# Weights of the merge and output products split once, ahead of the last stage, and its first inputs loaded before it begins

## The chip, the cores and the metric

One core of a Trainium2 chip (five engines: PE or TensorE, DVE or VectorE, ACT or ScalarE, POOL or GpSimd, SP or SyncE, and 16 DMA engines that serve the queues of SP and ACT). The metric is the device time of one execution in microseconds; less is better.

## The reference

One layer of a decoder trunk over 2048 tokens and 1024 channels, in float32. The input is normalised and modulated, projected to 8704 columns, and these columns feed four mixers (pooling, a gated linear recurrence, a short convolution, differential attention) and their gates. What follows is the part that the last stage of the kernel computes:

```python
gates = jax.nn.sigmoid(m_g.reshape(B_, T, N_BRANCH, D))
merged = (gates[:, :, 0] * (y_pool @ w_merge_pool[l])
          + gates[:, :, 1] * (y_hgrn @ w_merge_hgrn[l])
          + gates[:, :, 2] * (y_conv @ w_merge_conv[l])
          + gates[:, :, 3] * (y_diff @ w_merge_diff[l]))
out = merged @ w_out[l]
x = x + gate[:, None] * rmsnorm(out, g_post[l])
```

The branch outputs have 256, 256, 256 and 512 channels, ten blocks of 128 together.

## The kernel before, in words

**Split products.** Every large product is made from operands that are split in two: a high part, rounded to PE's fast 32-bit format (an ACT copy), and a low part, the rest (a DVE or POOL subtraction). Three products stand for one: high by high, high by low, low by high.

**The trunk** (`trunk`, from L124) makes the input projection. Its work is cut into 476 products in slots 0 to 475, twelve matmuls of 128x512 each (L1682 to L1684), 238 for each half of the tokens. In the first half the weights of `w_in` are loaded by SP (`load_w1`, `load_w2`) into `w1` and `w2_0`, `w2_1`, split by ACT (`high`) and DVE (`low`) and stored; in the second half ACT only reloads the stored parts (L933), so `w1` and `w2` have no user there. Each engine has one program, a loop over the slots that is written out, with the mixers and the attention placed in it by slot numbers (second half: attention from slot 284 over 71 slots). A result leaves PSUM by ACT (L949) or DVE (L1250) and SP stores it, gates into the scratch tensor `gT` (L414), branch outputs into `yT`. At the end SP waits until all is stored, and a barrier of all engines parts the trunk from the last stage.

**The last stage** (`merge_and_output`, L1906) goes over four groups of 512 tokens. A group has eight merge steps `d`, one for each 128 channels of the merged result, and then four output blocks `b` of 128 tokens.

In a merge step PE makes 30 matmuls into four PSUM banks, one for each branch (L2222 to L2224): ten blocks of the branch output `y` by the weights `wm` of this `d`, three products each. DVE multiplies each bank with its gate (L2095), POOL adds the four (L2054, L2056), ACT copies the high part of the sum (L2154, `high`), DVE subtracts for the low part (L2084, `low`). DVE's order is fixed: `low(n - 1)` stands between the second and the third multiplication of step `n`. So a step's last two multiplications wait for the POOL and ACT work on the step before.

The weights of a step are loaded anew in every group, four DMAs of rows of 512 bytes, 0.66 MB together (L1977), two buffers, two steps ahead; ACT and DVE split them again each time (`split_wm`: L2130, L2075). The gates of a step are one DMA of 1.05 MB (L1985) in rows of 2 KB out of four planes of `gT` that lie 8 MB apart; four buffers, sigmoid on ACT (L2148).

In the first group `w_out` comes in besides (`load_wo`, L1997), eight blocks of 0.5 MB, split by ACT (L2166) and POOL (L2059); the first output product waits for the last of them.

An output block is 48 matmuls (L2208 to L2210) into one of two banks `pb`. ACT takes the mean square (L2183) and its root, DVE scales (L2113), POOL adds `x` (L2064), SP stores. The ten `y` blocks of the next group are loaded one after the other (L1991, two buffers), from the last merge step on, and split by ACT and DVE (L2144, L2080); four of these splits stand ahead of the last `high` and `low` in both programs:

```python
if not last:
    for k in range(4):
        split_y(g + 1, k)
low(KD * g + KD - 1, KD - 1)
```

and PE's block 0 uses six of the eight merged parts before it needs that last `low`.

## Time and profile before

| | us |
|---|---|
| median of 3 runs | 2531.88 (2531.22 to 2540.31) |
| the profiled execution | 2534.88, its span 2533.1 |
| last product of the trunk ends, first product of the last stage starts | about 2031.4, 2044.9 |
| group 0 of the last stage: merges, output | 102.6, 47.8 |
| group 1 | 60.0, 53.0 |
| group 2 | 59.7, 53.2 |
| group 3 | 59.6, 43.7, and 8.6 to the end of the span |

The profile has a row for each instruction with its start and its duration, the idle time of the engine before it and what ended it. Its windows give, for a stretch of time, the busy time of each engine, the granted share of TensorE's full clock (PEclk: 1.00 is 2.4 GHz, 0.50 is 1.2 GHz) and the share of time in which the 16 DMA engines moved packets (overlapping packets make it a little more than 1).

### The profile page before, as it was taken

What the parts mean: (1) busy time and instruction counts of PE and PEld (TensorE: products, weight loads), DVE (VectorE), ACT (ScalarE), POOL (GpSimd) and SP (SyncE); (2) the same over time, 40 slices, a digit from 0 to 9 for tenths busy, and PEclk for the clock granted to TensorE, in tenths of its full rate; (3) what the DMA queues carried; (4) which work ended last, traced back from release to release, by engine and by line L of the source; (5) the groups of instructions that cost most, each with busy time, mean ns of one, the idle gap of its engine ahead of it and who ended that gap; (6) DMA issues with size and microseconds to landing.
All of it is one profiled execution on the core that took longest, in us unless ns stands there. A gap on an engine that the chain in (4) does not pass through costs nothing. (4 is left out here: it accounts for less than half of the span.)

```text
span 2533.1 us, 35157 instructions
## 1 busy us (share of the span) xinstructions
PE 2274.4 (90%) x11572; PEld 1871.5 (74%) x11572; DVE 1434.6 (57%) x2638; ACT 1144.1 (45%) x2400; POOL 839.4 (33%) x739
## 2 busy tenths in 40 slices
PE   3698799998999889898999999999999966989898
PEld 2486677777777668687888888878888844767676
DVE  5676566655888777312766666445556334444442
ACT  3553455543544543422666666434434233434341
POOL 0113223223745645200222222124343225244353
PEclk7799999999999989999999999999999988999999
DMA  6799777757767667989464654588777676576581
GB/s 227 260 352 328 259 231 241 223 204 277 264 239 261 230 222 253 332 265 264 163 191 146 181 169 149 171 258 250 230 247 235 213 238 178 155 190 187 148 226 61
DMA packets 383963, 564.75 MB, mean 223 GB/s; under 512 B 32432, under 2 KB 248880, under 8 KB 382768
## 3 DMA queue, kind: packets, MB, share of 16 engines
q1 hardware_dynamic: 315248, 313.01, 42.0%
q10 hardware_dynamic: 68544, 249.59, 27.8%
q8 instruction: 91, 1.49, 0.2%
q14 instruction: 80, 0.66, 0.1%
HBM read 331.28 MB, written 231.21 MB: 222 GB/s over the span
## 5 line engine op out<-in xcount | busy, mean ns | idle before, releaser
L1682 PE MATMUL gb<-h_hi,w_both 128*128 128x512 f32 x1904 | 789.0, 414 | 87.2 <-ACT o L949 41.7
L1684 PE MATMUL gb<-h_hi,w_both 128*128 128x512 f32 x1904 | 757.7, 398 | 0.0
L1683 PE MATMUL gb<-h_lo,w_both 128*128 128x512 f32 x1904 | 756.7, 397 | 0.0
L1682 PEld LDWEIGHTS gb<-h_hi,w_both 128*128 128x128 f32 x1904 | 366.9, 193 | 171.2 <-issue 91.7
L1684 PEld LDWEIGHTS gb<-h_hi,w_both 128*128 128x128 f32 x1904 | 365.7, 192 | 81.2
L1683 PEld LDWEIGHTS gb<-h_lo,w_both 128*128 128x128 f32 x1904 | 367.7, 193 | 67.1
L949 ACT ACTIVATE o<-gb 128x512 f32<-128x512 f32 x272 | 161.4, 594 | 372.5 <-PE gb L1684 308.0
L809 POOL TENSOR_TENSOR C_prob<-C_prob,C_cf 128x512 f32<-128x512 f32 (+3 forms) x160 | 156.9, 1005 | 506.1 <-DVE C_cf L1358 492.1
L1014 ACT ACTIVATE C_prob<-C_sc,C_negm 128x512 f32<-128x512 f32 (+3 forms) x320 | 198.5, 622 | 246.6 <-DVE C_negm L1336 239.9
L1250 DVE TENSOR_TENSOR o<-gb,o 128x512 f32<-128x512 f32 x204 | 140.3, 688 | 231.0 <-PE gb L1684 220.0
L1240 DVE TENSOR_TENSOR w_both<-w,w_both 128x512 fp32r<-128x512 f32 x170 | 142.1, 836 | 171.5 <-ACT w_both L922 171.1
L1336 DVE TENSOR_REDUCE C_negm<-C_sc 128x1 f32<-128x512 f32 (+3 forms) x320 | 179.7, 603 | 53.0 <-PE C_sc L1749 47.2
L2222 PE MATMUL D_mb<-D_y_hi,D_wm_hi 128*128 128x512 f32 x320 | 131.7, 411 | 50.5 <-DVE D_gate L2095 31.1
L1774 PEld LDWEIGHTS C_ob<-C_v_tok,C_at 128*128 128x128 f32 x1088 | 142.8, 191 | 32.9 <-issue 23.1
L1774 PE MATMUL C_ob<-C_v_tok,C_at 128*128 128x128 f32 x1088 | 148.6, 276 | 17.5 <-DVE C_y_out L1380 17.5
L2054 POOL TENSOR_TENSOR D_gate<-D_gate 128x1024 f32<-128x1024 f32 x32 | 98.1, 3066 | 178.8 <-DVE D_gate L2095 178.8
L922 ACT ACTIVATE w_both<-w 128x512 fp32r<-128x512 f32 x170 | 106.8, 628 | 103.2 <-DVE w_both L1240 55.6
L1368 DVE SCALAR_TENSOR_TENSOR C_prob<-C_prob,C_cf 128x512 f32<-128x512 f32 (+3 forms) x160 | 134.2, 840 | 2.3 <-POOL C_prob L809 2.2
L1748 PE MATMUL C_sc<-C_ks,C_qt 128*128 128x512 f32 (+3 forms) x320 | 119.8, 374 | 13.2 <-DVE C_causal_r L1330 10.6
L781 POOL TENSOR_TENSOR s<-w 128x512 f32<-128x512 f32 x34 | 48.3, 1422 | 248.7 <-DMA w<-in_w_in_dram 214.2
L2223 PE MATMUL D_mb<-D_y_lo,D_wm_hi 128*128 128x512 f32 x320 | 128.2, 401 | 0.0
L2224 PE MATMUL D_mb<-D_y_hi,D_wm_lo 128*128 128x512 f32 x320 | 127.8, 399 | 0.0
(230 smaller groups left out, 3722.6 us busy)
## 6 DMA issues: line engine op xcount, KB each, us to landing
wS_scratch<-w_both ACTq DMA_DIRECT2D x238, 512.0 KB, 4.4
w_both<-wS_scratch ACTq DMA_DIRECT2D x238, 512.0 KB, 4.3
w<-in_w_in_dram SPq DMA_DIRECT2D x68, 512.0 KB, 5.2
gT_scratch<-o SPq DMA_DIRECT2D x128, 256.0 KB, 4.6
D_gate<-gT_scratch SPq DMA_DIRECT2D x32, 1024.0 KB, 9.8
pT_scratch<-o SPq DMA_DIRECT2D x80, 256.0 KB, 4.2
C_qt<-qB_scratch SPq DMA_DIRECT2D x128, 128.0 KB, 3.4
C_ks<-kT_scratch SPq DMA_DIRECT2D x48, 256.0 KB, 5.7
```

What stands on the lines that cost most here:

```text
L809: tt(second, second, cf[i % 3][:, 1, p:p + 1].to_broadcast([P, width(z)]), ALU.mult).then_inc(scaled, 1)
L949: a(o[b][:, :], gb[n % 2][:, :], ACT.Copy).then_inc(copied, 1)
L1014: a(prob[z % PROBS][:, m, 0:width(z)], sc[(2 * z + m) % 3][:, 0:width(z)], ACT.Exp, bias=negm[i % 2][:, m, p:p + 1], accum_out=sums[i % 2] ...
L1240: tt(w_lo[n % RING][:, :, :], source(n), w_hi[n % RING][:, :, :].bitcast(F32), ALU.subtract).then_inc(wlo, 1)
L1250: tt(o[b][:, :], gb[n % 2][:, :], o[c][:, :], ALU.add).then_inc(summed, 1)
L1336: nc.vector.tensor_reduce(negm[i % 2][:, m, p:p + 1], sc[(2 * z + m) % 3][:, 0:width(z)], AX.X, ALU.max, negate=True).then_inc(max_ready, 1)
L1368: stt(first_map, first_map, cf[i % 3][:, 0, p:p + 1], prob[z % PROBS][:, 1, 0:width(z)], ALU.mult, ALU.add).then_inc(a_ready, 1)
L1682: mm(to, hi[:, k, :], h_hi[j][:, k, :], start=(fresh and k == 0), stop=False, skip_group_check=True)
L1683: mm(to, hi[:, k, :], h_lo[j][:, k, :], start=False, stop=False, skip_group_check=True)
L1684: last = mm(to, lo[:, k, :], h_hi[j][:, k, :], start=False, stop=(k == KH - 1), skip_group_check=True)
L1774: last = mm(ob[i % 2][:, 0, :], at[z % 2][:, y, :], v_tok[:, 4 * p + y, :], start=(z == begin[i] and y == 0), stop=(p == 0 and y == nb - 1))
L2222: mm(mb[b][:, :], wm_hi[d % 2][:, k, :], y_hi[:, k, :], start=(k == c0), stop=False)
```

## The change

Four things are changed.

1. **Splits.** In slots 286 to 461 of the trunk, every fifth slot takes one of 36 half rows (128x512) of the four merge weights and of `w_out`: SP loads it into the free `w1` three slots earlier, ACT copies the high part in that slot, DVE subtracts the low part, SP stores both one slot later into two new scratch tensors: `wmS`, one contiguous 1.31 MB piece for each `d` (10 KB a partition), and `woS`, 1.05 MB for each of eight blocks (8 KB a partition). The last stage loads both parts ready-made, one DMA each; its ACT, DVE and POOL splits of weights are gone.
2. **First inputs.** The buffers of the first `y` blocks, of `wm` 0 and 1 and of gates 0 and 1 exist through the trunk. During its last seven products SP loads them: after product 469 two `y` blocks, then eight `y` blocks in two DMAs, `wm` 0, gates 0, `wm` 1, and after the last product gates 1. SP waits for all of them before the barrier.
3. **When weights are loaded.** A buffer of `wm` is free only when PE has used it (`merged_done` of the step two back); before, it was free once split. Gates go ahead of `wm` in SP's order. The eight loads of `w_out` follow each `wm` load of the first group.
4. **Order of the output products.** Block 0 and block 1 both use six of eight merged parts first, then both the last two; blocks 2 and 3 are as before.

```diff
+SPLITS, APART, BLOCKS = 286, 5, 36
+            def load_block(k):
+                sp.wait_ge(wlo, KEPT + max(0, k - 1))
...
+                sp.dma_start(block_in[k % 2], src).then_inc(w2_loaded[k % 2], 16)
+            def store_block(k):
+                sp.wait_ge(wlo, KEPT + k + 1)
...
+            def load_last(p):
+                sp.wait_ge(product_done, PRODUCTS - PER + p + 1)
...
+                if p == 0:
+                    for k in range(2):
+                        load(l_y_stage[k][:, :], yT[k, :, 0:TG])
+                if p in (1, 2):
+                    load(l_gate[p + 1][:, :, :], yT[4 * p - 2:4 * p + 2, :, 0:TG].rearrange("n p t -> p n t"))
+                if p in (3, 5):
+                    d = (p - 3) // 2
+                    load(l_wm[d][:, :, :, :].bitcast(F32).rearrange("p l k c -> p (l k c)"), wmS[d].rearrange("p l k c -> p (l k c)"))
+                if p in (4, 6):
+                    d = (p - 4) // 2
+                    load(l_gate[d][:, :, :], gT[d:d + 3 * KD + 1:KD, :, 0:TG].rearrange("n p t -> p n t"))
...
             mixers_over(1)
+            sp.wait_ge(last_loaded, 16 * 8)
...
+            def high_block(k):
+                act.wait_ge(w2_loaded[k % 2], 16 * (NU // 2 + k // 2 + 1))
+                if k >= 2:
+                    act.wait_ge(block_stored[k % 2], 16 * STORES[k - 2])
+                a(block_both[k % 2][:, 0, :].bitcast(F32R), block_in[k % 2], ACT.Copy).then_inc(whi, 1)
...
             def load_wm(n, d):
-                if not (isinstance(n, int) and n < 2):
-                    sp.wait_ge(wm_hi_ready, n - 1)
-                    sp.wait_ge(wm_lo_ready, n - 1)
-                for w, (c0, c1) in zip(w_merge, BRANCH_CHUNKS):
-                    sp.dma_start(wm_stage[d % 2][:, c0:c1, :], w[0, :, d * P:(d + 1) * P].rearrange("(k p) n -> p k n", p=P)).then_inc(wm_loaded[d % 2], 16)
+                sp.wait_ge(merged_done, 4 * (n - 1))
+                sp.dma_start(wm_both[d % 2][:, :, :, :].bitcast(F32).rearrange("p l k c -> p (l k c)"),
+                             wmS[d].rearrange("p l k c -> p (l k c)")).then_inc(wm_loaded[d % 2], 16)
...
                     if not (last and d + 2 >= KD):
+                        load_gates(n + 2, (d + 2) % KD, at if d + 2 < KD else at_next)
                         load_wm(n + 2, (d + 2) % KD)
-                        load_gates(n + 2, (d + 2) % KD, at if d + 2 < KD else at_next)
-                    if first and d + NW < KD:
-                        load_wo(d + NW)
+                    if first:
+                        load_wo(d)
...
+                if first:
+                    pe.wait_ge(wo_loaded, 16 * KD)
+                for b in range(2):
...
+                    for half in range(2):
+                        for k in range(KD - 2):
+                            output(g, b, half, k)
+                pe.wait_ge(m_lo_ready, KD * g + KD)
+                for b in range(2):
+                    for half in range(2):
+                        for k in range(KD - 2, KD):
+                            done = output(g, b, half, k)
+                    done.then_inc(p_done, 1)
```

SP's program where the trunk ends and the last stage begins (line 414 stores a gate tile; 621 a branch output), before:

```order
L621 DMA yT_scratch<-B_yh 128x2x128
L414 DMA gT_scratch<-o 128x512 x3
L133 UNCONDITIONAL_BRANCH
L1965 UNCONDITIONAL_BRANCH
L1991 DMA D_y_stage<-yT_scratch 128x512 x2
L1977 DMA D_wm_stage<-in_w_merge_pool_dram 128x2x128
L1977 DMA D_wm_stage<-in_w_merge_hgrn_dram 128x2x128
L1977 DMA D_wm_stage<-in_w_merge_conv_dram 128x2x128
L1977 DMA D_wm_stage<-in_w_merge_diff_dram 128x4x128
L2033 DMA D_gate<-yT_scratch 128x4x512 x2
L1985 DMA D_gate<-gT_scratch 128x4x512
```

and now:

```order
L468 DMA D_wm_both<-wmS_scratch 128x2560
L492 DMA gT_scratch<-o 128x512
L468 DMA D_gate<-gT_scratch 128x4x512
L492 DMA gT_scratch<-o 128x512 x2
L160 UNCONDITIONAL_BRANCH
L2055 UNCONDITIONAL_BRANCH
L2111 DMA D_post<-post_scratch 128x1024
L2073 DMA D_gate<-gT_scratch 128x4x512
L2064 DMA D_wm_both<-wmS_scratch 128x2560
L2081 DMA D_wo_both<-woS_scratch 128x2048
L2073 DMA D_gate<-gT_scratch 128x4x512
L2064 DMA D_wm_both<-wmS_scratch 128x2560
```

The first loads of the last stage stand ahead of the barrier (the two branches), with the trunk's last stores behind a load of gates; after it come, for each step, gates, `wm` and one block of `w_out`.

ACT's program in a slot of the trunk with a split (line 1107 is an exponential of the attention, 1026 reloads stored weights of `w_in`), now; before, the row L1015 was not there:

```order
L1128 ACTIVATE C_rstd<-C_ssq 128x1
L1026 DMA w_both<-wS_scratch 128x1024
L1015 ACTIVATE w_0<-w 128x512
L1107 ACTIVATE C_prob,C_sums<-C_sc,C_negm 128x512
L1120 ACTIVATE C_at<-C_tb 128x512
```

The copy stands ahead of the attention's next exponential.

## Rows read from the trace of the kernel before

**Rows 1.** The page: busy time of each engine in the span

```profile
PE 2274.4 (90%) x11572; PEld 1871.5 (74%) x11572; DVE 1434.6 (57%) x2638; ACT 1144.1 (45%) x2400; POOL 839.4 (33%) x739
```

**Rows 2.** The windows: stretch, its length, busy time of each engine (instructions), PEclk, DMA share, GB/s

```profile
1800.00:2030.00 230.00, 230.00 (x1279) 186.59 (x1278) 114.00 (x263) 87.48 (x152) 77.41 (x98) 1.00 0.74 230
...
2031.80:2044.90 13.10, 0.00 (x0) 0.00 (x0) 2.94 (x4) 2.81 (x5) 0.00 (x0) 0.68 0.72 239
2044.90:2147.50 102.60, 66.83 (x240) 49.87 (x240) 49.81 (x54) 40.90 (x39) 51.53 (x24) 0.87 0.77 210
2147.50:2195.30 47.80, 46.32 (x192) 37.83 (x193) 14.13 (x15) 13.64 (x25) 7.55 (x3) 0.95 0.41 116
2195.30:2255.30 60.00, 56.04 (x241) 44.59 (x240) 33.30 (x44) 29.95 (x26) 35.19 (x15) 1.00 0.96 241
2255.30:2308.30 53.00, 46.19 (x193) 37.71 (x192) 16.32 (x18) 14.12 (x26) 11.33 (x6) 0.94 0.40 115
...
2421.20:2480.80 59.60, 55.92 (x242) 44.55 (x241) 33.30 (x44) 30.06 (x26) 35.23 (x15) 1.00 0.78 205
2480.80:2524.50 43.70, 43.70 (x193) 35.80 (x191) 6.44 (x7) 7.38 (x15) 11.02 (x6) 1.00 0.24 72
```

**Rows 3.** The waits from 1260 to 2030 us: total us, times, longest

```profile
ACT o L949 <- PE gb L1684: 153.9, 65, 7.7
...
DVE o L1250 <- PE gb L1684: 126.0, 58, 8.7
```

**Rows 4.** The timeline at the two ends of the first merges: start, us, instruction, idle before

```profile
2034.88 0.82 SPq L1991 DMA_DIRECT2D D_y_stage<-yT_scratch  x2
...
2044.93 0.80 PE L2222 MATMUL D_mb<-D_y_hi,D_wm_hi 128*128 128x512 f32 x1 [13.60 <-DVE D_wm_lo L2075]
```

**Rows 5.** The timeline where the first output products start

```profile
2147.55 0.80 PE L2208 MATMUL D_pb<-D_wo_hi,D_m_hi 128*128 128x512 f32 x1 [10.16 <-POOL D_wo_lo L2059]
```

**Rows 6.** The timeline, ACT and DVE where the third group starts

```profile
2310.22 1.28 ACT L2148 ACT_TABLE_LOAD   x1
2310.24 1.28 DVE L2113 SCALAR_TENSOR_TENSOR D_o_buf<-D_pb,D_rstd,D_post 128x1024 f32<-128x1024 f32 x1 [7.50 <-ACT D_rstd L2187]
2311.52 1.92 ACT L2148 ACTIVATE D_gate<-D_gate 128x2048 f32<-128x2048 f32 x1
```

**Rows 7.** Line 2054: duration ns min/median/max, first and last start

```profile
L2054 POOL TENSOR_TENSOR D_gate<-D_gate x32: 2337/3582/3598, 2063.4 to 2483.6; 128x1024 f32<-128x1024 f32 x32
```

**Rows 8.** The timeline of two merge steps of the second group, POOL's rows

```profile
2244.08 3.59 POOL L2054 TENSOR_TENSOR D_gate<-D_gate 128x1024 f32<-128x1024 f32 x1 [2.67 <-DVE D_gate L2095]
...
2247.75 1.28 POOL L2056 TENSOR_TENSOR D_gate<-D_gate 128x512 f32<-128x512 f32 x1
...
2251.70 2.40 POOL L2054 TENSOR_TENSOR D_gate<-D_gate 128x1024 f32<-128x1024 f32 x1 [2.67 <-DVE D_gate L2095]
```

**Rows 9.** The timeline, end of the second group's merges

```profile
2262.83 1.19 ACT L2144 ACTIVATE D_y_hi<-D_y_stage 128x512 fp32r<-128x512 f32 x2 [6.70 <-DMA D_y_stage<-yT_scratch]
...
2270.46 0.80 PE L2208 MATMUL D_pb<-D_wo_hi,D_m_hi 128*128 128x512 f32 x1 [6.81 <-DVE D_m_lo L2084]
```

**Rows 10.** The windows: the stretch behind that wait

```profile
2270.40:2274.00 3.60, 3.54 (x8) 2.81 (x9) 0.70 (x2) 1.13 (x2) 0.00 (x0) 0.50 0.48 137
```

**Rows 11.** The DMA view, 2133.3 to 2140.3 us: one gate load alone

```profile
DMA packets 528, 1.05 MB, mean 150 GB/s; under 512 B 16, under 2 KB 16, under 8 KB 528
...
q1 hardware_dynamic: 528, 1.05, 71.9%
```

**Rows 12.** The DMA view, 2041.5 to 2046.5 us: loads of branch outputs

```profile
DMA packets 996, 1.97 MB, mean 394 GB/s; under 512 B 31, under 2 KB 36, under 8 KB 996
...
q1 hardware_dynamic: 996, 1.97, 104.8%
```

**Rows 13.** The page: split of a weight block on DVE (busy, mean ns); DMA issues (KB, us to landing)

```profile
L1240 DVE TENSOR_TENSOR w_both<-w,w_both 128x512 fp32r<-128x512 f32 x170 | 142.1, 836 | 171.5 <-ACT w_both L922 171.1
...
w_both<-wS_scratch ACTq DMA_DIRECT2D x238, 512.0 KB, 4.3
```

More of the change, by code:

```diff
@@ L66, with last_inputs, block_at @@
 MIX_BASE = [130 + 12 * i for i in range(8)] + [372 + 25 * i // 2 for i in range(8)]
+BRANCH_CHUNKS = ((0, 2), (2, 4), (4, 6), (6, 10))
+YC = 10
+GB = 4
+def last_inputs(sb):
+    y_stage = [sb(f"y_stage{j}", [P, TG]) for j in range(2)]
+    late_gates = [sb(f"gate{j}", [P, 4, TG]) for j in range(2, GB)]
+    y_first = [y_stage[k] if k < 2 else late_gates[(k - 2) // 4][:, (k - 2) % 4, :] for k in range(YC)]
+    wm_both, gate = [], []
+    for j in range(2):
+        wm_both.append(sb(f"wm_both{j}", [P, 2, YC, P], F32R))
+        gate.append(sb(f"gate{j}", [P, 4, TG]))
+    return wm_both, gate + late_gates, y_stage, y_first
+def block_at(slot, offset):
+    k, r = divmod(slot - SPLITS - offset, APART)
+    return k if r == 0 and 0 <= k < BLOCKS else None
 def column(u):
@@ L1527, in _ @@
                     low(n + LEAD)
+                k = block_at(n, 0)
+                if k is not None:
+                    low_block(k)
                 if n == 0:
@@ L1928, in merge_and_output @@
         m_lo = sb("m_lo", [P, KD, TG], F32R)
-        gate = [sb(f"gate{j}", [P, 4, TG]) for j in range(GB)]
         x_in = sb("x_in", [P, D])
@@ L1953, in merge_and_output @@
         block = ctx.enter_context(nc.Block())
-        wo_v = w_out.rearrange("a (k p) n -> p (a k) n", p=P)
         TB = TG // P
@@ L2180, in body @@
                     act.wait_ge(scaled, n)
-                    if first:
-                        act.wait_ge(wo_lo_ready, KD)
-                    a(wo_stage[:, :], pb[b % 2][:, :], ACT.Square, accum_out=ss[:, :]).then_inc(squared, 1)
+                    a(square[:, :], pb[b % 2][:, :], ACT.Square, accum_out=ss[:, :]).then_inc(squared, 1)
                     act.wait_ge(squared, n + 1)
@@ L2214, in body @@
                     n = KD * g + d
-                    pe.wait_ge(wm_lo_ready, n + 1)
+                    if not (first and d < 2):
+                        pe.wait_ge(wm_loaded[d % 2], 16 * (KD // 2 * g + d // 2))
                     for b, (c0, c1) in enumerate(BRANCH_CHUNKS):
@@ L2225, in body @@
+                            mm(mb[b][:, :], wm_both[d % 2][:, 0, k, :], y_lo[:, k, :], start=False, stop=False)
+                            done = mm(mb[b][:, :], wm_both[d % 2][:, 1, k, :], y_hi[:, k, :], start=False, stop=(k == c1 - 1))
                         done.then_inc(merged_done, 1)
                 if first:
-                    pe.wait_ge(wo_lo_ready, KD)
-                for b in range(TB):
-                    n = TB * g + b
-                    if not (first and b < 2):
-                        pe.wait_ge(scaled, n - 1)
+                    pe.wait_ge(wo_loaded, 16 * KD)
@@ L2232, in body @@
+                for b in range(2):
+                    if not first:
+                        pe.wait_ge(scaled, TB * g + b - 1)
                     if b == 0:
                         pe.wait_ge(m_lo_ready, KD * g + KD - 2)
-                        for half in range(2):
-                            for k in range(KD - 2):
-                                output(g, b, half, k)
-                        pe.wait_ge(m_lo_ready, KD * g + KD)
-                        for half in range(2):
-                            for k in range(KD - 2, KD):
-                                done = output(g, b, half, k)
-                    else:
-                        for half in range(2):
-                            for k in range(KD):
-                                done = output(g, b, half, k)
+                    for half in range(2):
+                        for k in range(KD - 2):
+                            output(g, b, half, k)
@@ new lines, in body @@
+                pe.wait_ge(m_lo_ready, KD * g + KD)
[4 more added lines that the diff above has]
+                    done.then_inc(p_done, 1)
+                for b in range(2, TB):
+                    pe.wait_ge(scaled, TB * g + b - 1)
+                    for half in range(2):
+                        for k in range(KD):
+                            done = output(g, b, half, k)
```

147 lines of the change are left out of this document (67 added, 80 removed).

## The prediction

> **What bounds the kernel now.** The page [rows 1] gives PE 90%, so I ask where the other tenth is. The windows [rows 2] show it: in the trunk's second half PE is busy all the time at full clock; in the last stage it is not. PE's own need there is read from the last output stretch, 193 matmuls in 43.7 us, 0.227 us each: 6.8 us for a merge step of 30, 54.4 us for eight, 43.6 us for an output of 192, 98 us a group. Group 0 takes 150.4, groups 1 and 2 take 113, group 3 takes 103.3. Four causes stand in the rows:
>
> - PE idles 13.6 us between trunk and last stage [rows 4]; the last stage's first DMA is issued at 2034.9, and its data and splits fill the rest.
> - Group 0's merges take 102.6 us, and the first output product waits 10.2 us more for the last split of `w_out` [rows 5].
> - Merges of groups 1 to 3 take some 60 us. In a late step POOL's first addition takes 3.6 us beside DVE's weight split and 2.4 us without it [rows 7, 8]. With 1.3 for the second addition and the 2.7 that POOL idles before the next step's (`high`, `low` and two multiplications run in it) that makes 7.6, the distance of the two POOL rows [rows 8].
> - At the end of a group `y` loads are waited for, and PE stands 6.8 us [rows 9], then runs at 0.50 of the clock for 3.6 us and more [rows 10]: the output takes 53.0 us instead of 43.6, so 2.6 to 2.8 is the clock's part.
>
> The column to keep in mind is DMA in groups 1 and 2: 0.96 busy during merges [rows 2]. That is the next bound.
>
> **What a step of loads costs.** One gate load alone, 1.05 MB, keeps the engines 71.9% busy over 7.0 us [rows 11]: 5.0 us of engine time. Rows of the same 2 KB from `yT` run at 394 GB/s with 104.8% shown [rows 12], so gates are slow by themselves, not for their row length. A step before has 0.96 x 7.5 = 7.2 us of engine time: 5.0 gates and 2.2 for 0.66 MB of weights. Now the weights are both parts, 1.31 MB in long rows; I take 394 GB/s, 3.3 us. Since full engines show 1.05, 5.0 of gates take 4.8 us. A step is 8.1 us of DMA against 6.8 of PE. Bounds: gates at 3.5 (300 GB/s, towards rows 12), 6.8 together; all at the 241 GB/s that merges show now [rows 2], 9.8. I take 8.1 because it comes from the same tensor in the same stage.
> [...]
>
> **The change part by part.**
>
> *Trunk splits.* 36 ACT copies and 36 DVE subtractions of 128x512, 0.6 [rows 9] and 0.84 us [rows 13], and 28 MB of traffic over 175 slots. ACT waits 154 us for PE's products and DVE 126 us [rows 3], over 2 us each time, in the stretch where they run, and PE has no gap: hidden. Reloads of stored weights land in 4.3 us [rows 13], three slots ahead. Without cover it would be 36 x 1.5 = 53 us. I take +2.
>
> *Preloads.* SP now waits for them before the barrier. Products end at 2031.4 and take 2.7 us each, so `wm` 0 is issued at 2023.3. A reload of 0.52 MB lands after 4.3 us [rows 13], 1.3 of them transfer: 3.0 us fixed. Then 2023.3 + 3.0 + 3.3 (`wm` 0) + 4.8 + 3.3 + 4.8 (gates 0, `wm` 1, gates 1) + 3.3 for five gate-tile stores in between = 2045.8, against 2034.9: 11 us later. From there ACT's ten copies (6.3), table load and sigmoid (3.2) [rows 6] and the last subtraction (0.8) lead to the last twelve matmuls of step 0, 2.7; with 0.5 between them step 1 starts 13.5 us on, 2059.3.
>
> *Group 0.* Each step loads `w_out` too, 1.05 MB at 394 GB/s, 2.6 us: 10.7 us a step, all on one queue, in SP's order `wm`, `w_out`, gates. `wm` may be issued only when PE is done with the step two back. From step 1's start: step 3 starts at 3.0 + 10.7 + 3.3 = 17.0, four more at 10.7, and step 7 runs 6.8: merges end 66.6 later, 2125.9. Then the queue still holds, from step 7's start, 3 x 2.6 + 2 x (4.8 + 3.3) = 24.0, of which PE covers 6.8: the last `w_out` block, behind the `wm` that waits for step 7, lands 17.2 later. Output starts at 2143.1 (2147.5 now). With 43.6, 2.8 for the clock after the wait and 0.6 (below) it ends at 2190.1 against 2195.3: **-5.2**.
>
> *Groups 1 to 3, merges.* DVE's weight split and ACT's go, so POOL's addition takes 2.4 in every step and the ring becomes 2.4 + 1.3 + 2.7 = 6.4, below PE's 6.8. But DMA sets the pace: 6.9 for step 0, then 3.0 + 2 x 8.1 + 3.3 = 22.5 to step 4, 1.3 for an output store, 3 x 8.1, and 6.8 = 61.8, against 60.0, 59.7 and 59.6: +1.8, +2.1, +2.2. The removed work is paid back in bytes.
>
> *Outputs.* `y` loads now stand in SP's queue behind a `wm` load that waits for PE's last merge step. From step 7's start 2 x 8.1 + 1.3 (`x`) + 1.3 (two `y`) = 18.8; less 6.8, 12.0 after merges; from first `y` to PE's product 7.6 [rows 9]: 19.6. The new order gives PE 72 matmuls first, 16.3: a wait of 3.3. I add half of the clock's 2.8 as the wait is half as long. Block 2 now follows block 0's end by one quarter block, 2.7 us; square, root and scaling take 3.2 (output ends at 2308.3 [rows 2], scaling at 2311.5 [rows 6]), so with a step between them 0.6. 48.9 against 53.0 and 53.2, and +0.6 in group 3: **-4.1, -4.3, +0.6**.
>
> Sum: -5.2, group 1 -2.3, group 2 -2.2, group 3 +2.8, trunk +2: **-4.9 us**. It is made against the profiled execution, 2534.9, which is 3 us above the median; taken off the median 2531.9 it gives 2527.
>
> **The rivals.** *B: DMA keeps up.* Gates are slow only where small rows and waits mix in; a step of loads is 6.8 or less. Then merges are PE's, 55.2 us, outputs 44.2: groups 1 to 3 give -13.6, -13.5, -3.8. Group 0: preloads 2.6 shorter, merges end 60.1 after 2056.7, output 14.6 later, end 2178.4: -16.9. With +2: -46, **2486**. For: 2 KB rows do run at 394 GB/s [rows 12]. Against: rows 11, a gate load with nothing beside it.
> The Trainium skill (HBM Reference, Specifications) gives a core about 358 GB/s; a step's 2.36 MB would take 6.6 us by it, which is B's result. No row of gates shows that rate.
>
> *C: DMA is worse than 8.1, slower.* Mechanism: doubling the weight bytes makes the queue the bound of every merge step. At 241 GB/s a step takes 9.8: merges 73.3 in groups 1 to 3 (+13.5 each), outputs +2.5, +2.3, +0.6, group 0 +28.6 (`w_out` 4.4 a step, start 2051.2): +77, 2608. Between 8.1 and 9.8 one microsecond of the step is worth 48, so it decides from 8.5 on; the middle of the case is 8.9, **2565**. For: 0.96 busy today. Against: long rows should beat 512 bytes.
>
> *D: the trunk's splits show.* ACT's copy stands before an exponential and DVE's subtraction waits for it; if half of 53 us reaches PE, +26: **2553**. Against: rows 3.
>
> *That the change does not do what it says* on the stall at the group's end is in A already: 3.3 us of it stay.
>
> **How the numbers follow.** A, as summed, with steps from 7.8 to 8.4 us: 2518 to 2541, chance 0.50. B 0.27, C 0.16, D 0.07. A measurement of this kernel can tell about 0.5%, 12.7 us: 2519.2 to 2544.5 is no change. A gives 0.12 faster, 0.33 same, 0.05 slower; B 0.27 faster; C 0.16 slower; D 0.02 same, 0.05 slower. Faster 0.39, same 0.35, slower 0.26. The range reaches from B's value to the middle of C, 2484 to 2566; A's own stands beside it.
>
> **What would show it.** Right: DMA share about 1.0 in merges of groups 1 and 2 with steps near 8 us, PE released by the `wm` load; POOL's first addition 2.4 throughout; first product of the last stage near 2048; a wait of some 17 us before group 0's output. B would show steps of 6.8 and waits of a few us there. C would show steps of 9 and more. D would show PE gaps between 1300 and 2030. The forecast is wrong if a gate load alone takes much less than 7 us, or if PE's order of blocks 0 and 1 leaves no wait at all.

## The result, and the profile after

The changed kernel takes **2540.39 us** (median of 20 runs, 2532.32 to 2546.65) against 2534.44 for the kernel before beside it (20 runs, 2527.06 to 2540.31). The ratio is 1.0023, 95% interval 1.0014 to 1.0032: 6 us slower, where 4.9 us faster was forecast. By the bound of 0.5% that is no change, and it lies within the range, but the sign is wrong and the interval leaves it no doubt. The profiled execution took 2532.32 us (span 2530.5), the fastest of the 20. Its slot 286, ahead of which only the first loads of the splits run, starts at 1197.3 us, that of the kernel before at 1203.6. Such a difference of two executions is as large as the effect, so stages are compared here, not ends.

The page of the changed kernel first: its engines, PE's first merge product, POOL's first addition and three of its loads.

```profile
PE 2270.2 (90%) x11572; PEld 1867.7 (74%) x11572; DVE 1409.5 (56%) x2642; ACT 1116.6 (44%) x2396; POOL 803.6 (32%) x731
...
L2262 PE MATMUL D_mb<-D_y_hi,D_wm_both 128*128 128x512 f32 x320 | 133.8, 418 | 56.0 <-DMA D_wm_both<-wmS_scratch 33.7
L2126 POOL TENSOR_TENSOR D_gate<-D_gate 128x1024 f32<-128x1024 f32 x32 | 76.6, 2394 | 219.9 <-DVE D_gate L2158 219.9
...
D_wm_both<-wmS_scratch SPq DMA_DIRECT2D x32, 1280.0 KB, 9.5
D_gate<-gT_scratch SPq DMA_DIRECT2D x32, 1024.0 KB, 13.3
```

All engines work a little less than in [rows 1], POOL's addition is 2.4 us everywhere (3.58 in the middle of [rows 7]), and what PE waits for is now the weight load. The windows of the last stage's eight parts, in the columns of [rows 2]:

```profile
2051.30:2144.60 93.30, 63.23 (x241) 48.85 (x241) 30.35 (x47) 23.52 (x23) 29.39 (x16) 0.85 0.86 304
2144.60:2191.00 46.40, 45.98 (x193) 37.54 (x194) 13.02 (x14) 12.64 (x24) 7.58 (x3) 0.95 0.34 94
2191.00:2255.70 64.70, 58.62 (x241) 46.97 (x240) 26.27 (x39) 22.09 (x20) 28.23 (x15) 0.95 0.92 287
2255.70:2301.50 45.80, 44.17 (x193) 35.88 (x192) 12.94 (x15) 12.54 (x24) 11.18 (x5) 1.00 0.52 156
2301.50:2365.30 63.80, 57.30 (x242) 45.83 (x241) 26.17 (x39) 21.96 (x20) 28.23 (x15) 0.97 0.92 295
2365.30:2410.00 44.70, 44.12 (x194) 35.88 (x193) 13.26 (x15) 12.54 (x24) 11.19 (x5) 1.00 0.48 153
2410.00:2477.60 67.60, 59.79 (x241) 47.73 (x240) 26.32 (x39) 21.96 (x20) 28.18 (x15) 0.92 0.76 241
```

Merges of groups 1 to 3 grew from 60.0, 59.7 and 59.6 us to 64.7, 63.8 and 67.6; outputs of groups 1 and 2 shrank from 53.0 and 53.2 to 45.8 and 44.7. Now PE's gaps: the timeline of its rows with idle time ahead of them, in group 0 and in two places of groups 1 and 2 (start, duration, instruction, idle before it and what ended it).

```profile
2080.43 0.65 PE L2262 MATMUL D_mb<-D_y_hi,D_wm_both 128*128 128x512 f32 x1 [4.37 <-DMA D_wm_both<-wmS_scratch]
2091.68 0.50 PE L2262 MATMUL D_mb<-D_y_hi,D_wm_both 128*128 128x512 f32 x1 [2.57 <-DMA D_wm_both<-wmS_scratch]
2103.24 0.80 PE L2262 MATMUL D_mb<-D_y_hi,D_wm_both 128*128 128x512 f32 x1 [4.46 <-DMA D_wm_both<-wmS_scratch]
...
2144.57 0.79 PE L2247 MATMUL D_pb<-D_wo_both,D_m_hi 128*128 128x512 f32 x1 [15.80 <-DMA D_wo_both<-woS_scratch]
...
2224.69 0.49 PE L2262 MATMUL D_mb<-D_y_hi,D_wm_both 128*128 128x512 f32 x1 [2.21 <-DMA D_wm_both<-wmS_scratch]
...
2273.38 0.50 PE L2247 MATMUL D_pb<-D_wo_both,D_m_hi 128*128 128x512 f32 x1 [1.17 <-DVE D_m_lo L2149]
```

The stall at the end of a group, 6.81 us in [rows 9], is 1.17 us; in its place stand waits of up to 3.3 us within the merges, three of over 1 us in each of groups 1 to 3. Last, the turn from trunk to last stage, in SP's, DVE's, ACT's and PE's rows.

```profile
2027.28 0.33 SPq L468 DMA_DIRECT2D D_wm_both<-wmS_scratch  x1
...
2030.00 0.38 SPq L468 DMA_DIRECT2D D_gate<-gT_scratch  x1
...
2030.43 3.49 SPq L492 DMA_DIRECT2D gT_scratch<-o  x2
2049.15 0.33 SPq L2111 DMA_DIRECT2D D_post<-post_scratch  x1
2049.21 0.06 DVE L2140 MEMSET D_epsb<- 128x1 f32 x1 [21.22 <-PEq L160]
2049.30 1.15 ACT L2191 ACTIVATE D_y_hi<-D_y_stage 128x512 fp32r<-128x512 f32 x2 [18.69 <-DVE D_epsb L2140]
...
2051.31 0.80 PE L2262 MATMUL D_mb<-D_y_hi,D_wm_both 128*128 128x512 f32 x1 [21.34 <-DVE D_y_lo L2145]
```

PE stands 21.3 us there, 13.6 in [rows 4]. The last stores of gates are issued at 2030.4, behind the preloads in the same queue, and the last stage begins at 2049.2.

### The profile page after: what moved, and what is told of

The parts are those of the page before. It is cut to its first block and busy times, and to the rows that moved or that the text cites. A ratio compares the mean times of both kernels' runs of the same rounds, so it can differ in the third digit from the quotient of the medians.

```text
span 2530.5 us, 35114 instructions
## 1 busy us (share of the span) xinstructions
PE 2270.2 (90%) x11572; PEld 1867.7 (74%) x11572; DVE 1409.5 (56%) x2642; ACT 1116.6 (44%) x2396; POOL 803.6 (32%) x731
## 5 line engine op out<-in xcount | busy, mean ns | idle before, releaser
L2262 PE MATMUL D_mb<-D_y_hi,D_wm_both 128*128 128x512 f32 x320 | 133.8, 418 | 56.0 <-DMA D_wm_both<-wmS_scratch 33.7
L2126 POOL TENSOR_TENSOR D_gate<-D_gate 128x1024 f32<-128x1024 f32 x32 | 76.6, 2394 | 219.9 <-DVE D_gate L2158 219.9
L2263 PE MATMUL D_mb<-D_y_lo,D_wm_both 128*128 128x512 f32 x320 | 130.6, 408 | 0.0
L2264 PE MATMUL D_mb<-D_y_hi,D_wm_both 128*128 128x512 f32 x320 | 130.1, 407 | 0.0
## 6 DMA issues: line engine op xcount, KB each, us to landing
D_gate<-gT_scratch SPq DMA_DIRECT2D x32, 1024.0 KB, 13.3
```

What stands on the lines that cost most here:

```text
L2262: mm(mb[b][:, :], wm_both[d % 2][:, 0, k, :], y_hi[:, k, :], start=(k == c0), stop=False)
L2263: mm(mb[b][:, :], wm_both[d % 2][:, 0, k, :], y_lo[:, k, :], start=False, stop=False)
L2264: done = mm(mb[b][:, :], wm_both[d % 2][:, 1, k, :], y_hi[:, k, :], start=False, stop=(k == c1 - 1))
```

## The experiments

Each kernel ran beside the kernel before on the same chip; ratios are to it. "The stretch" is the time from the first product of slot 286 to the trunk's last product (827.7 us before, 832.7 in the changed kernel), "the gap" PE's idle time behind it. The changed kernel itself was run once more: ratio 1.0025 (1.0014 to 1.0036), 2536.66 us, stretch 833.6, gap 20.3, merges of groups 1 to 3 62.5, 64.4, 62.4. So parts of one kernel differ by up to 5 us between executions; differences below that are read only from medians or from many equal rows.

**No trunk splits.** The 36 blocks are neither loaded nor split nor stored; the last stage reads as many bytes of other stored weights, so its output is not the product.

```
-                k = block_at(n, -3)
-                if k is not None:
-                    load_block(k)
...
-                k = block_at(n, 0)
-                if k is not None:
-                    high_block(k)
```

> The changed kernel without the 36 loads, splits and stores in the trunk; the last stage loads blocks of the same size and layout out of the stored weights of the input projection instead (so its result is another one). T: within 4 us of the changed kernel, about 2537 to 2541. S: 8 us or more below it, about 2530, and PE's gaps in the trunk's second half go.

Ratio 0.9988 (0.9975 to 1.0001), 2527.43 us: 9 us below the changed kernel beside it. The stretch falls to 827.3. So the splits cost 5 to 6 us in their own stretch, not 2. Without them the ratio lies below 1, though its interval just reaches it. The other 3 us of the medians have no place in the two traces that I could name.

**Half the weight bytes.** In `load_wm` only the high parts are loaded again, the low ones stay as the first loads left them. The output lacks the right low parts.

```
-                sp.dma_start(wm_both[d % 2][:, :, :, :].bitcast(F32).rearrange("p l k c -> p (l k c)"),
-                             wmS[d].rearrange("p l k c -> p (l k c)")).then_inc(wm_loaded[d % 2], 16)
+                sp.dma_start(wm_both[d % 2][:, 0, :, :].bitcast(F32).rearrange("p k c -> p (k c)"),
+                             wmS[d, :, 0].rearrange("p k c -> p (k c)")).then_inc(wm_loaded[d % 2], 16)
```

> The changed kernel with each weight load of the last stage behind the preloads bringing only the high part, 0.66 MB instead of 1.31 (the low part stays that of the preload, so the result is another one). T: a step's loads fall from 8.1 to about 6.5 us, below PE's 6.8; groups 1 to 3 fall from about 110 to 101 to 103 us, group 0 by 5 to 10, the total to about 2505 to 2512. S, or a rival (P) in which only the later start of the last stage costs: no more than 6 us less than the changed kernel.

Ratio 0.9842 (0.9826 to 0.9857), 2488.72 us, 48 less than the changed kernel. Merges of groups 1 to 3 take 55.6, 55.4 and 56.1. That bytes set the pace is right; I had expected 2505 to 2512 us, and what I left out is that PE's clock comes back with them. The windows over the second group's merges in this kernel:

```profile
2186.00:2241.00 55.00, 54.37 (x239) 44.41 (x238) 22.73 (x35) 15.82 (x13) 29.34 (x16) 1.00 0.91 259
```

**Contiguous gates.** The changed kernel with gates stored as a step reads them, four tiles side by side in a row of 8 KB, in place of four planes 8 MiB apart.

```
-    gT = nc.dram_tensor("gT_scratch", [GATE_TILES, P, T], F32).ap()
+    gT = nc.dram_tensor("gT_scratch", [KD, NG * P, 4, TG], F32).ap()
...
-... gT[d:d + 3 * KD + 1:KD, :, bass.ds(at, TG)].rearrange("n p t -> p n t")).then_inc(g_loaded
+... gT[d, bass.ds(at, P), :, :]).then_inc(g_loaded
```

> The changed kernel with the gates stored so that the load of one step is one contiguous piece (8 KB a partition) in place of four planes 8 MB apart; the trunk's stores become rows of 2 KB that lie 8 KB apart, same bytes. T: a gate load falls from about 5 to 2.6 us of DMA time, a step's loads to 5.9 us; merges run at PE's pace, groups 1 to 3 take 99 to 101 us, the first product of the last stage comes 4 us earlier, total 2485 to 2500. If gates were slow only for the traffic beside them (my rival B), the layout changes nothing: within 5 us of the changed kernel.

Ratio 0.9814 (0.9796 to 0.9832), 2480.58 us: 56 us below the changed kernel. The page's two rows of loads, then the windows over the second group's merges and output:

```profile
D_wm_both<-wmS_scratch SPq DMA_DIRECT2D x32, 1280.0 KB, 6.7
...
D_gate<-gT_scratch SPq DMA_DIRECT2D x32, 1024.0 KB, 9.0
```

```profile
2166.00:2221.50 55.50, 55.16 (x242) 44.81 (x241) 26.55 (x39) 22.33 (x20) 28.32 (x15) 1.00 0.89 339
2221.50:2265.80 44.30, 43.84 (x193) 35.95 (x192) 13.40 (x15) 12.53 (x24) 11.18 (x5) 1.00 0.49 155
```

The same bytes come in 9.0 us instead of 13.3, the queue moves 339 GB/s instead of 287 at a lower share, and PE is busy 55.2 of 55.5 us. So a step of 8.1 us takes both, the slow layout of the gates and the doubled weights: with either taken away, here or in the run before, merges take 55 to 57 us. This edit makes the rows longer and takes the planes away at once; that the distance of the planes counts and not the 2 KB row is argued from [rows 12], where rows of 2 KB out of planes 1 MiB apart moved at 394 GB/s. The Trainium skill (DMA: Bandwidth & Descriptors, Latency and other measured facts) advises to pad a row pitch of 4 or 8 MiB or to lay tiles out contiguously; it measured 103 GB/s at such a pitch between the rows of neighbouring partitions and 214 with the pitch padded. Here those rows lie 8 KB apart and only the planes 8 MiB, which is another case, but the advice holds in it: 339 GB/s against 287.

**Contiguous gates in the kernel before**, nothing of the change.

> The kernel before with gates kept contiguous by step, nothing of the change. Theory S (the slow gate loads matter to the changed kernel because they and the doubled weights share the queue, while the kernel before is paced by POOL's addition beside DVE's split, 7.6 us a step): DMA share in merges falls from 0.96 to about 0.7, merges of groups 1 to 3 stay at 57 to 60 us, output's wait for y shrinks; the time falls by 5 to 15 us, far less than the 56 that the same edit gives the changed kernel. Rival T (the gates bound the kernel before as well): merges fall to 55 to 56 and the time by 35 us or more.

Ratio 0.9952 (0.9938 to 0.9965), 2519.01 us, 12.4 us less than before. Gate loads land in 6.1 us, and the merges of groups 1 to 3 stay at 59.5 to 59.6 us. POOL's additions still follow each other every 7.6 us, and so do PE's steps:

```profile
2198.29 3.58 POOL L2055 TENSOR_TENSOR D_gate<-D_gate 128x1024 f32<-128x1024 f32 x1 [2.67 <-DVE D_gate L2096]
2201.95 1.29 POOL L2057 TENSOR_TENSOR D_gate<-D_gate 128x512 f32<-128x512 f32 x1
2205.91 3.58 POOL L2055 TENSOR_TENSOR D_gate<-D_gate 128x1024 f32<-128x1024 f32 x1 [2.67 <-DVE D_gate L2096]
```

With contiguous gates the change is worth some 35 us by the ratios (0.9952 and 0.9814), 38 by the medians. With the planes it is worth nothing: each of the two edits takes away one of two bounds that stood close behind each other.

**Output products in the old order**, block 0 whole, then block 1.

```
-                for b in range(2):
...
+                for b in range(TB):
+                    n = TB * g + b
...
+                        pe.wait_ge(m_lo_ready, KD * g + KD - 2)
+                        for half in range(2):
+                            for k in range(KD - 2):
+                                output(g, b, half, k)
+                        pe.wait_ge(m_lo_ready, KD * g + KD)
```

> Output products in the old order, block 0 first in both halves and all row blocks, the rest as in the changed kernel. Theory S (the new order covers the wait for y at the end of groups 0 to 2): PE waits some 10 us in the first output of each of groups 0 to 2 instead of 2 to 4, and runs at half clock behind it, outputs of groups 1 and 2 take 54 to 58 us instead of 45 to 46; +8 to +11 each, and together the kernel is 15 to 25 us slower than the changed one. Rival T (the loads are the bound, so a wait in the output only lets the queue catch up and merges get shorter by as much): outputs longer but merges of groups 1 to 3 shorter by as much, time within 5 us.

Ratio 1.0084 (1.0067 to 1.0101), 2553.52 us, 15 us above the changed kernel by the ratios (0.6%). In groups 1 and 2 PE stands 19.9 us in two waits for the last merged columns, 12.8 the longest, and outputs of groups 1 and 2 take 58.5 and 53.1. The clock's part can be read in this kernel's windows, the first of these two outputs ahead of the second:

```profile
2260.00:2318.50 58.50, 45.74 (x193) 37.39 (x192) 13.68 (x16) 12.32 (x24) 11.16 (x5) 0.88 0.44 135
...
2384.60:2437.70 53.10, 45.95 (x193) 37.49 (x193) 13.63 (x15) 12.28 (x24) 11.18 (x5) 0.94 0.42 130
```

The merges do not get shorter for it (63.9, 66.1, 66.6). The order of products is the part of the change that earns.

**No preloads.** The same first loads are issued behind the barrier.

```
-                if 0 <= n - PRODUCTS + PER - 1 < PER:
-                    load_last(n - PRODUCTS + PER - 1)
...
+            for p in (0, 3, 1, 2, 4, 5, 6):
+                load_last(p)
```

> The same first loads are issued after the barrier, in the order y, first weights, y, y, gates, weights, gates. Theory S (the preloads' gain is nearly all lost since the barrier waits for their landing and group 0 is a queue of bytes): barrier at about 2034, first product of the last stage at 2044 to 2047 as before (13 to 16 us behind the last product), but step 1 as late as in the changed kernel or up to 6 us later; the time is within 5 us of the changed kernel. Rival T (preloads take 5 MB off the queue of group 0, which is worth their transfer time): 5 MB at 300 GB/s is 16 us later.

Ratio 1.0043 (1.0025 to 1.0061), 2541.5 us. The interval overlaps that of the changed kernel (1.0014 to 1.0036). The first product comes 11.8 us after the trunk's last, but the merges of group 0 take 103.6 us: output starts 115.4 us after the trunk, 114.6 with preloads. What the preloads buy as they stand is not clear of the noise: 0.8 us in the traces, some 5 by the ratios.

**Waits moved.** The trunk doesn't wait for the preloads; ACT and PE wait for each of them where they use it.

```
-                    sp.dma_start(to, src).then_inc(last_loaded, 16)
+                    sp.dma_start(to, src).then_inc(early[p], 16)
...
-            sp.wait_ge(last_loaded, 16 * 8)
...
+                if start:
+                    act.wait_ge(early[0 if k < 2 else 1 + (k - 2) // 4], 32 if k < 2 else 16)
```

> The trunk no longer waits for the preloads before the barrier; the first users in the last stage do. Theory S (the last stage is a queue of loads from its first us on, and the preloads delay only its start): the gap between the trunk's last product and the last stage's first falls from 21 us to about 12 to 14, the first w_out and gate loads are issued 8 to 11 us earlier, and the kernel is 6 to 10 us faster than the changed one. Rival T (group 0 is bound by the queue's bytes from the preloads on, so an earlier first product only waits longer for the second weights): the gap falls but output of group 0 starts less than 3 us earlier, and the time changes by less than 3 us.

Ratio 1.0017 (1.0005 to 1.0029), 2535.32 us, the same as the changed kernel. My theory falls: the gap is 21.55 us, as wide as before the edit, and output starts 115.7 us after the trunk. SP now waits for its last gate stores alone, and these stand in the queue behind 4.7 MB of preloads. In the changed kernel's trace the last preload lands at 2047.3 us and the last store at 2048.7, so the wait that was taken away had ended 1.3 us ahead of the one that stayed. That gives the next experiment.

**Stores first.** As the last kernel, and the second weights and gates are issued behind those stores.

```
-                if 0 <= n - PRODUCTS + PER - 1 < PER:
+                if 0 <= n - PRODUCTS + PER - 1 < 5:
                     load_last(n - PRODUCTS + PER - 1)
...
             mixers_over(1)
+            load_last(5)
+            load_last(6)
```

> As e_waits_moved, and the last two preloads (second weights, second gates, 2.4 MB) are issued behind the last stores of gates instead of ahead of them. Theory S (the barrier waits for those stores, which stand on the same queue behind 4.7 MB of preloads, and not for the preloads themselves, which is why moving the waits alone brought nothing): the gap between the trunk's last product and the last stage's first falls from 21 us to 12 to 15, and the kernel is 3 to 8 us faster than the changed one. Rival T (the gap is made by the number of bytes in the queue, whichever stands first, or step 1 then waits for the second weights as long as the gap shrank): the gap falls but step 1 starts as late after the last product as now, 31 us or more, time within 2 us.

Ratio 0.9984 (0.9973 to 0.9996), 2527.73 us, some 10 us below the changed kernel. Timeline of the turn:

```profile
2030.07 5.30 SPq L493 DMA_DIRECT2D gT_scratch<-o  x3
...
2042.23 0.33 SPq L469 DMA_DIRECT2D D_wm_both<-wmS_scratch  x1
...
2044.84 0.32 SPq L2113 DMA_DIRECT2D D_post<-post_scratch  x1
...
2047.10 0.76 PE L2270 MATMUL D_mb<-D_y_hi,D_wm_both 128*128 128x512 f32 x1 [12.72 <-DVE D_y_lo L2147]
```

The gap is 12.7 us, and output of group 0 starts 106.4 us after the trunk instead of 114.6. What held the barrier was the stores' place in the queue behind the loads. This version beats the kernel before, by 0.2%.

**Low split later.** DVE's subtraction one slot after ACT's copy, the stores one slot later too.

```
-                k = block_at(n, 0)
+                k = block_at(n, 1)
                 if k is not None:
                     low_block(k)
```

> Theory S (the trunk's splits cost about 5 us, because DVE stands 1.7 us for ACT's copy at each of 36 splits and the addition and exponential behind it come late): with DVE's subtraction one slot later ACT's copy is done when DVE comes to it; the waits of line 1340 for line 1015 (61 us in 36) fall below 10, the stretch from slot 286 to the last product falls from 832.7 to 828 or 829, and the kernel is 3 to 5 us faster than the changed one. Rival T (the loss comes from ACT's copy ahead of the exponential, or from the traffic, not from DVE's standing): the waits go but the stretch stays within 1 us of 832.7 and the time within 2 us.

Ratio 1.0028 (1.0014 to 1.0042), 2537.59 us: nothing gained. DVE no longer stands, but the stretch is 837.1, longer by 4.5. The new loss is at slots 360 to 363, where the mixers start, 6.3 us over the kernel before instead of 2.1: there DVE waited 10.8 us for ACT's eviction, and ACT 14.2 us in two waits for stores of earlier tiles to free its buffers (11.3 in the changed kernel, 9.8 before). SP, which issues them, had meanwhile got one more wait ahead of them; that this is the reason is not tested.

The total hides what the attention's slots say. The changed kernel loses 0.87, 0.56, 0.34 and 0.47 us in slots 296, 306, 316 and 336, the same in both of its traces; here all four lose 0.00, though ACT's copy stands where it stood. Slots 286 to 288 lose 1.9 us instead of 0.5. DVE's rows ahead of slot 306 show why, first in the changed kernel, then in this one:

```profile
1326.83 0.69 DVE L1350 TENSOR_TENSOR o<-gb,o 128x512 f32<-128x512 f32 x1 [1.65 <-PE gb L1787]
1327.92 0.69 DVE L1340 TENSOR_TENSOR w<-w,w 128x512 fp32r<-128x512 f32 x1 [0.40 <-ACT w L1015]
1328.53 1.28 DVE L1436 TENSOR_REDUCE C_negm<-C_sc 128x1 f32<-128x512 f32 x2
```

```profile
1335.97 0.69 DVE L1350 TENSOR_TENSOR o<-gb,o 128x512 f32<-128x512 f32 x1 [1.65 <-PE gb L1787]
1336.58 1.28 DVE L1436 TENSOR_REDUCE C_negm<-C_sc 128x1 f32<-128x512 f32 x2
```

The reductions give the maximum that ACT's next exponential waits for. They start 1.70 us behind the start of DVE's eviction in the changed kernel and 0.61 in this one. What these four slots pay for is thus DVE's subtraction, with its wait for the copy, ahead of the reductions, and not the copy ahead of the exponential. So the theory was right for four of the five slots, and the edit lost more elsewhere than it gained there.

**Splits placed elsewhere.** 20 blocks in slots 243 to 281, two slots apart, 16 in slots 380 to 455.

```
-SPLITS, APART, BLOCKS = 286, 5, 36
+BLOCKS = 36
+BLOCK_SLOTS = [243 + 2 * k for k in range(20)] + [380 + 5 * k for k in range(16)]
```

> The 36 trunk splits leave the attention and the start of the mixers: 20 of them 2 slots apart in slots 243 to 281, 16 of them 5 apart in slots 380 to 455, all else as in the changed kernel. Theory S (the 5 us of the trunk are lost where ACT's copy stands before the attention's exponentials, slots 286 to 336, and where the mixers start, about slot 360, whose stores and loads crowd SP's queue): the stretch from slot 286 to the last product falls from 832.7 to 827 to 829, slots 238 to 286 stay within 1 us, and the kernel is 4 to 6 us faster than the changed one. Rival T (the cost is the 28 MB of traffic and 36 operations wherever they stand): the stretch from slot 238 to the last product stays as long as in the changed kernel, time within 2 us.

Ratio 1.0090 (1.0074 to 1.0106), 2555.16 us: 17 us worse. The stretch gains a little (831.3), and slots 238 to 286 lose 22, 151.6 to 173.8 us. The windows over most of them, first of the kernel before, then of this one:

```profile
1055.00:1200.00 145.00, 134.83 (x596) 110.14 (x595) 30.68 (x45) 39.76 (x64) 9.47 (x4) 0.98 0.90 279
```

```profile
1055.00:1200.00 145.00, 128.17 (x550) 102.81 (x548) 38.91 (x56) 43.75 (x73) 6.43 (x3) 0.96 1.04 344
```

The engines have time to spare (DVE 39, ACT 44 of 145 us), but the DMA queues were 0.90 full and are 1.04 full with the splits' traffic; PE then waits for ACT's evictions, 20.0 us in seven waits in these slots against 7.9 in three in the changed kernel, and those evictions for stores to free ACT's buffers, 43.0 us against 24.0. The rest of the 22 us is in PE's own time, 148.0 us busy against 141.5 at a clock of 0.94 against 0.99. I had read the idle engines and not the queue.

**Operations only.** The 36 copies and subtractions stay in their slots, loads and stores are left out, and the last stage reads other stored weights.

```
-                act.wait_ge(w2_loaded[k % 2], 16 * (NU // 2 + k // 2 + 1))
                 if k >= 2:
-                    act.wait_ge(block_stored[k % 2], 16 * STORES[k - 2])
+                    act.wait_ge(wlo, KEPT + k - 1)
```

> The 36 copies and 36 subtractions of the trunk stay in their slots, their 36 loads and 56 stores are left out, and the last stage reads other stored weights. Theory S (two costs: ACT's copy ahead of the attention's exponentials, 2.8 us in slots 286 to 336, and SP's fuller queue where the mixers start, slots 360 to 363, about 2): the attention's losses stay, those of slots 360 to 363 go; the stretch from slot 286 to the last product is 830 to 831, against 827.5 without splits and 832.7 with all of it. Rival T (all of it is traffic): 827 to 828. Rival U (all of it is the engines' operations): 832 to 833.

Ratio 0.9993 (0.9980 to 1.0005), 2532.17 us. The stretch is 831.2. Against the kernel before, the same five slots lose as in the changed kernel (286: 0.52, 296: 0.80, 306: 0.50, 316: 0.32, 336: 0.47 us, 2.6 together), and slots 360 to 363 lose 0.3 instead of 2. So the two costs in the stretch are apart: half is the two operations in the attention (by e_low_later DVE's, in four of the five slots), half is traffic where the mixers start. The medians divide otherwise: this ratio is as low as that of the kernel without splits (0.9988), as if the operations cost next to nothing. The profiled execution is the slowest of its 11, and the stretch alone can't settle it; how the 9 us of the medians divide stays open. Below are PE's waits in the stretch from 1195 to 1660 us in the changed kernel, then without splits (total, times, longest).

```profile
PE C_sc L1851 <- ACT C_prob L1107: 3.5, 6, 1.3
PE gb L1785 <- ACT o L1042: 2.4, 1, 2.4
PE C_tb L1865 <- DVE C_prob L1468: 1.4, 2, 1.2
PE gb L1785 <- DVE o L1350: 1.2, 1, 1.2
```

```profile
PE C_sc L1836 <- ACT C_prob L1098: 2.1, 4, 0.8
PE C_tb L1850 <- DVE C_prob L1456: 1.2, 1, 1.2
PE gb L1770 <- DVE o L1338: 0.5, 1, 0.5
```

PE's waits sum to 8.5 against 3.8 us.

**All together.** Contiguous gates, waits moved, stores first, and two blocks of `w_out` loaded right behind the barrier; first with the splits placed elsewhere, then in the changed kernel's slots.

```
             sp.dma_start(post[:, :], post_d).then_inc(post_loaded, 16)
+            for k in range(2):
+                load_wo(k)
...
-                    if first:
-                        load_wo(d)
+                    if first and d < 6:
+                        load_wo(d + 2)
```

> All together: contiguous gates, waits for preloads moved behind the barrier, last two preloads behind the stores, splits placed as in e_splits_placed, two of the w_out blocks loaded right behind the barrier. Theory S (the parts are independent): 2480.6 less 5 (trunk), less 3 to 5 (gap, 15.7 to about 12), less 2 to 5 (group 0's wait for w_out): 2464 to 2471. Rival T (with fast gates the gap is no longer made by the queue and group 0 is bound by the w_out bytes in any order): only the trunk's 5 are left, 2474 to 2478.

> e_best with the splits back in the changed kernel's slots. Theory S (moving them into slots 243 to 281 cost some 20 us there since the queue was full already, and all else in e_best works by itself): slot 238 to 286 falls from 170 to 152 us, the stretch behind it rises by 3, the gap stays at 10 to 12 and group 0's merges at 65 to 66; 2464 to 2469 us. Rival T (e_best's short merges of group 0 come from something that the placing did): merges of group 0 are 70 or more, 2472 or more.

The first: ratio 0.9814 (0.9799 to 0.9828), 2483.23 us, the placing eats what the rest gains. The second: ratio **0.9740** (0.9727 to 0.9753), **2467.31 us**, 65 us below the kernel before. Windows over its merges of groups 0 and 1:

```profile
2045.00:2110.50 65.50, 59.35 (x241) 46.40 (x242) 29.56 (x46) 23.57 (x23) 25.84 (x14) 0.96 1.00 413
2156.20:2212.80 56.60, 55.04 (x241) 44.82 (x240) 26.55 (x39) 22.34 (x20) 28.29 (x15) 1.00 0.88 334
```

The gap is 10.7 us, merges of group 0 take 65.4 with the queue full, and what is left to gain in the last stage is the gap, 11 us of group 0 over PE's own 54.4, and some 2 us in the merges of each later group (56.6, 56.2 and 56.1).

## Why the prediction was wrong

The place of every effect was right, and the sign was not: the terms missed by 2 to 11 us each, partly against each other, on a sum of 4.9. With times after the trunk's last product, the profiled executions side by side:

| term | forecast | measured |
|---|---|---|
| trunk, the stretch | +2 | +5.0 (827.7 to 832.7) |
| group 0, to its output's end | -5.2 | -3.0 (164.0 to 161.0) |
| merges of groups 1 to 3 | +1.8, +2.1, +2.2 | +4.7, +4.1, +8.0 |
| outputs of groups 1 to 3 | -4.1, -4.3, +0.6 | -7.2, -8.5, +0.6 |
| sum | -4.9 | +3.7 |

The medians say +6; of the 2.3 between I have no row. Behind the trunk the forecast was -6.9; this trace gives -1.3 and the changed kernel's second one -3.9. So the last stage did get shorter, by less than was forecast, and the trunk took more than that back: +5.0 and +5.9 in the two traces.

*Trunk splits, the step that failed.* "PE has no gap: hidden" came from ACT's and DVE's waits for products, 154 and 126 us [rows 3]. Those are totals over 770 us and say nothing of where the waits stand: ahead of slot 306 DVE waits 1.65 us ahead of its eviction, and the subtraction comes behind it, where DVE has no time to spare. The windows of [rows 2], which show PE without a gap, begin at 1800 us, and the splits at 1197; there PE has waits of up to 1.2 us also in the kernel before, in the attention and where the mixers start, and the splits lengthen them (3.8 us together without splits, 8.5 with them). Measured were +5.0 us in the stretch in place of +2: 2.8 in five slots of the attention, where DVE's subtraction delays the maxima that the exponential needs (e_ops_only for the sum, e_low_later for DVE's part), and 2.1 in slots 360 to 363 by the splits' traffic (e_ops_only, e_no_splits). Rival D had DVE's wait for the copy in it, and a price five times too high. The trunk is not the whole of the wrong sign: with +2 in it the two traces would sum to +0.7 and -1.9, still short of -4.9, and the next term has the rest.

*Merges, the term that was mis-sized.* 61.8 us was 54.4 of PE and 7.4 of waits. The waits came as summed: in group 1 PE is idle 6.1 of 64.7 us, in group 2 6.5, in group 3 7.8. The step of 8.1 is borne out as a mean, 2.36 MB at 287 to 295 GB/s being 8.2 to 8.0, and 64.7 us for eight steps being 8.1; single steps of group 1 take 6.8 to 10.8. What I left out is that PE's own time doesn't stay 54.4: the same 241 matmuls were busy 56.0 us at a granted clock of 1.00 [rows 2], and are busy 58.6, 57.3 and 59.8 at 0.95, 0.97 and 0.92. I had charged the clock behind the long waits of an output and not behind waits of 1.8 to 3.3 us in merges. This is 7.7 us over three groups, more than the sum; the 1.6 by which 56.0 is over 54.4 makes 4.8 more. e_half_weights and e_gates_after, whose windows show 1.00, end 48 and 56 us below the changed kernel, more than I had expected from the queue's bytes alone.

*Outputs.* 48.9 us assumed 3.3 of waiting and 1.4 of clock; PE waits 1.17 for a merged part in group 1 and for none in group 2; that no wait is left was named as a sign of a wrong forecast. The second trace has one wait of 4.7 and an output of 50.8: the term is a near miss of two arrivals and differs between executions. e_old_order shows that the order carries it.

*Preloads.* The barrier was forecast at 2045.8 because SP waits for the preloads; it fell at 2049.2. The preloads had landed at 2047.3, and the last stores, which travel behind them, at 2048.7: the wait that ended last is for the stores. e_waits_moved took the other away and nothing moved; e_stores_first moved two loads behind the stores and took 8 us off. So the step named the wrong wait. The forecast came near because it counts the bytes of both, five stores among them, in one queue; that the two waits end so close together was not foreseen.

*Group 0.* A wait of 17.2 us for the last `w_out` block was forecast, 15.8 measured; output starts 114.6 us after the trunk, forecast 111.7 (2143.1 less 2031.4).

*The rivals.* B, DMA keeps up, did not come: gates are slow also with nothing beside them, as [rows 11] said. What it would give was priced well: with their layout changed the time is 2480.6, where B said 2486. C needed steps above 8.5 us and did not come.

## What to carry to other kernels

When precomputed data replaces work on an engine, price the bytes on the queue that they will share, in the stage where they are read and in the one where they are made; an idle engine beside a queue that is 0.9 full is no cover. When two bounds lie close together (here POOL at 7.6 us a step and the queue at 7.2), taking one away pays nothing until the other goes: both edits together gave 50 us where each alone gave 12 and nothing. Before a barrier, ask not only what is waited for but what stands ahead of it in the same queue. And where a total shows no gain, compare it slot by slot: an edit can gain in one place what it loses in another.

## What the runs showed of the hardware

Short waits cost PE more than their length. In groups 1 to 3 of the changed kernel PE has nine waits of over 1 us, 1.08 to 3.26. Within or just behind five of them, of 1.79 to 3.26 us, the granted clock falls to 0.50, its lower level, for some us; the other four, one of 2.85 us, pass without. So it averages 0.92 to 0.97 over 64 to 68 us. The windows behind two waits of the second group, of 2.08 us up to 2213.85 and of 1.79 up to 2247.18:

```profile
2214.00:2217.00 3.00, 3.00 (x8) 2.32 (x8) 1.22 (x3) 0.00 (x0) 1.89 (x1) 0.50 0.92 225
2217.20:2247.80 30.60, 26.60 (x117) 21.37 (x116) 12.54 (x20) 9.97 (x8) 12.68 (x8) 1.00 0.92 289
2248.00:2251.00 3.00, 3.00 (x8) 2.31 (x7) 0.83 (x2) 0.00 (x0) 2.70 (x2) 0.50 0.92 190
```

The kernel before, whose PE was idle 4 us of 60 in its second group's merges and never longer than 1.5, kept 1.00. Its longest wait there, in the timeline of the kernel before:

```profile
2203.75 0.50 PE L2222 MATMUL D_mb<-D_y_hi,D_wm_hi 128*128 128x512 f32 x1 [1.49 <-DVE D_gate L2095]
```

Rows of 2 KB in four planes 8 MiB apart moved at 150 GB/s [rows 11], and that load landed 8.0 us after its issue; the same bytes in rows of 8 KB, all but alone in the queue, landed after 4.8 us (e_gates_before). With them the DMA engines moved 413 GB/s over 65.5 us of e_best2's group 0, more than [rows 12] had shown. The Trainium skill (HBM Reference, Specifications) gives about 358 GB/s as a core's share and says that a core streaming alone measures well above it, about 425. This program runs on one core, and the 413 GB/s agree.

POOL's 128x1024 addition took 3.58 us beside DVE's splits and 2.39 without them, as [rows 8] had it for durations of 3.59 and 2.40.
